# Modulation strips that hold whole sums, and the last gate made in the router's stage

## The chip, the cores and the metric

One NeuronCore of one Trainium2 chip runs the whole kernel in a single launch. The metric is the time of one execution on the device in microseconds (us); less is better. Five engines work beside each other: PE (TensorE, matmuls; its weight loads are listed as PEld), DVE (VectorE), ACT (ScalarE), POOL (GpSimd) and SP (SyncE, whose queue issues almost all the loads). They wait for each other through semaphores only.

## The reference, cut to what matters

256 tokens of 1024 channels pass through one layer of a hybrid trunk. All data are float32.

```python
c_act = silu(c)                                   # c: (1, 1024)
mod = c_act @ ada_w + ada_b                       # (1, 6144)
sh1, sc1, gt1, sh2, sc2, gt2 = split(mod, 6)      # 1024 each
h = rms_norm(x, norm1_g) * (1 + sc1) + sh1
proj = h @ w_in                                   # q k v g gk_low z xbc dt gates: 11,312 columns in all
o_a = gla_mixer(...)                              # gated linear attention, chunks of 64
o_b = ssd_mixer(...)                              # causal conv of xbc, Mamba-2 scan, chunks of 64
merged = gate_a * (o_a @ w_oa) + gate_b * (o_b @ w_ob)
x = x + gt1 * (merged @ w_out)
h = rms_norm(x, norm2_g) * (1 + sc2) + sh2
x = x + gt2 * hier_moe(h, ...)                    # top-1 group of 4, top-2 of its 8 experts, SwiGLU, width 256
return rms_norm(x, final_norm_g)
```

The modulation is twelve blocks of 512 columns: 0 and 1 are sh1, 2 and 3 sc1, 4 and 5 gt1, 6 and 7 sh2, 8 and 9 sc2, 10 and 11 gt2.

## The kernel before, in words

**Weights** come in pieces of 1 MB (128 partitions x 2048 floats) in the order of the list `PIECES`. SP issues them in order (line 427) into a ring of five slots (`LOADS`), and each issue waits until the piece five places earlier has been used (`piece_used`). After them SP issues 96 expert pieces (three per expert, line 422) into sixteen slots (`moe_slots`): parts of buffers that are free by then, among them the eight ring slots. Expert piece j waits for the reader of piece j - 16. SP's queue is in order, so an issue that waits holds back all behind it.

**Split products.** A weight of the trunk is used as a rounded high part (ACT, line 567) and a low part (DVE, line 858), and each product is three matmuls in float32r. `SPLITS` lists the pieces that are split; a modulation piece is not. ACT and DVE split two pieces ahead of the point at which they stand (`AHEAD`, `before`).

**Order on PE.** The order is written out by hand: `sumsq`; the first four modulation blocks (`ADA_FIRST`, pieces loaded beside the ring into free buffers, `EARLY`); eight units `xbc` of 512 channels with the convolution on DVE; `k`, `q`, `v` (2), `g` (2), `z` (4), `gate` (4), `oa` (2), `ob` (2), `out` (2); the router; the experts. `project` does a unit: 96 matmuls of 256 columns where the output is channel-major, 48 of 512 where it is token-major (`k v g z out`). `ADA_AFTER` says behind which unit a modulation block stands. `keep_clock(n)` issues n matmuls of ones that nobody reads.

**A modulation block.** `modulation(i)` multiplies silu(c), repeated 32 times as a 32-column weight, with the two pieces of block i, 256 columns each. The eight k-steps of a piece go to four 32-row strips of one PSUM bank, so each strip holds the sum over two of the eight k-steps. ACT copies the bank to SBUF (`ada_out`, line 581). `modulation_columns(i)` then multiplies the copy by a column of ones in four matmuls, which adds the strips and turns the row into four columns of 128 channels; DVE scales these by 1/32 and adds `ada_b` (`modulation_out`, line 865). gt1 and gt2 are needed as rows: `modulation_rows(w)` makes diagonal matrices of the columns (DVE), PE multiplies ones by them (`gtb`), DVE copies. The rows of gt2 end in `gt2_two`, two halves of 64 rows, which scales the output of each expert.

**Small columns.** Behind `xbc` 0 PE makes `small`: the 16 columns of gk_low transposed (8 matmuls of 256 columns with a 16-column weight) and the 32 columns of dt (16 matmuls of 32 columns). `acum` (8 matmuls of 32 columns) and `gklin` (2 of 512 columns) stand behind `k`.

**Around the router.** After `out` 1 PE makes the logits, then `keep_clock(22)`; DVE works out the choices (lines 1183 to 1218) and releases `mask_ok`; PE makes `pos` (5 matmuls), `keep_clock(8)`, then `select_first_quad`, which gathers the rows of the first four experts, and `up_of(0)`. From there each expert is `up_of`, `turn_of`, `select_quarter`, `down_of`.

The small PSUM results (`MIX`) share banks 4 to 7 in turn, in the order of `PLAN`: `begin(name)` waits for the reader of the result four places earlier.

## Time and profile before

| | us |
|---|---|
| median of 3 runs (lowest to highest) | 741.28 (739.49 to 741.56) |
| the profiled execution, whole | 742.72 |
| its span in the trace | 740.9 |
| PE busy | 705.9 (95%) |
| DVE busy | 400.8 (54%) |
| ACT busy | 265.3 (36%) |
| mean traffic | 277 GB/s over the span |

The span is what the trace shows from the first to the last record of the core; 1.8 us of the execution lie around it.
### The profile page before, as it was taken

What the parts mean: (1) busy time and instruction counts of PE and PEld (TensorE: products, weight loads), DVE (VectorE), ACT (ScalarE), POOL (GpSimd) and SP (SyncE); (2) the same over time, 40 slices, a digit from 0 to 9 for tenths busy, and PEclk for the clock granted to TensorE, in tenths of its full rate; (3) what the DMA queues carried; (4) which work ended last, traced back from release to release, by engine and by line L of the source; (5) the groups of instructions that cost most, each with busy time, mean ns of one, the idle gap of its engine ahead of it and who ended that gap; (6) DMA issues with size and microseconds to landing.
All of it is one profiled execution on the core that took longest, in us unless ns stands there. A gap on an engine that the chain in (4) does not pass through costs nothing.

```text
span 740.9 us, 13185 instructions
## 1 busy us (share of the span) xinstructions
PE 705.9 (95%) x5600; PEld 570.0 (77%) x5600; DVE 400.8 (54%) x691; ACT 265.3 (36%) x375; POOL 66.6 (9%) x66
## 2 busy tenths in 40 slices
PE   9899999999999999999999999999999999997892
PEld 7689999989777777799998999886566666655541
DVE  3386778764675556997877456463423122121226
ACT  3245545547446244343635334222131122121001
POOL 0010000000000170440000000001111111111110
PEclk9998999999999999999999999999999999999997
DMA  9964647655776535334354447988999999999971
GB/s 367 416 220 178 236 169 284 229 187 220 256 281 228 192 118 173 132 126 136 113 196 148 171 168 270 423 341 313 407 416 418 418 421 420 420 419 420 420 296 58
DMA packets 30893, 200.48 MB, mean 271 GB/s; under 512 B 4999, under 2 KB 5383, under 8 KB 7410
## 3 DMA queue, kind: packets, MB, share of 16 engines
q1 hardware_dynamic: 27506, 193.01, 67.6%
q0 software_dynamic: 3328, 6.62, 2.4%
q8 instruction: 45, 0.74, 0.4%
q14 instruction: 14, 0.11, 0.0%
HBM read 194.57 MB, written 10.75 MB: 277 GB/s over the span
## 4 chain that ended last, share of the span: by engine, by line
PE 79%; DMA 11%; DVE 5%; ACT 2%; issue 2%; SPq 1%; DVEq 0%; ACTq 0%
PE ps L1446 77%; DMA ring<-in_expert_pieces 7%; DMA r_btm<-in_pieces 2%; DVE ring_rounded L858 1%; DMA ring<-in_pieces 1%; ACT ring_rounded L567 1%; PE ps L1566 1%; PE ps L1859 1%; SPq L422 1%; DVE r_kq L1067 0%; DVE r_xs_rounded L1130 0%; DVE x_sb L1402 0%; DVE x_sb L1429 0%; DVE x_sb L1421 0%; DVE r_kq L1061 0%
## 5 line engine op out<-in xcount | busy, mean ns | idle before, releaser
L858 DVE TENSOR_TENSOR ring_rounded<-ring,ring_rounded 128x2048 fp32r<-128x2048 f32 x60 | 138.0, 2304 | 91.4 <-ACT ring_rounded L567 91.2
L1446 PE MATMUL ps<-hT_rounded,ring_rounded 128*128 128x256 f32 x832 | 157.0, 289 | 0.9 <-DVE x_sb_rounded L897 0.9
L567 ACT CAST ring_rounded<-ring 128x2048 fp32r<-128x2048 f32 x60 | 114.2, 1904 | 70.2 <-DMA ring<-in_pieces 40.6
L1446 PEld LDWEIGHTS ps<-hT_rounded,ring_rounded 128*128 128x128 f32 x832 | 133.7, 196 | 4.1 <-issue 3.9
L1446 PE MATMUL ps<-x_sb_rounded,ring_rounded 128*128 128x256 f32 x416 | 119.4, 287 | 0.0
L1446 PE MATMUL ps<-ring_rounded,hT_rounded 128*128 128x512 f32 x352 | 109.5, 392 | 0.0
L1446 PEld LDWEIGHTS ps<-x_sb_rounded,ring_rounded 128*128 128x128 f32 x416 | 81.6, 196 | 0.2 <-issue 0.2
L1446 PEld LDWEIGHTS ps<-ring_rounded,hT_rounded 128*128 128x128 f32 x352 | 65.3, 188 | 14.9 <-issue 1.7
L1446 PE MATMUL ps<-ring,r_lm 128*64 128x256 f32 x512 | 65.4, 380 | 3.1 <-DMA ring<-in_expert_pieces 3.1
L1446 PEld LDWEIGHTS ps<-ring,r_lm 128*64 128x64 f32 x512 | 42.8, 137 | 27.1 <-issue 12.3
L788 ACT ACTIVATE sq<-ps 128x128 f32<-128x128 f32 x32 | 8.9, 277 | 147.9 <-PE ps L1446 147.9
L530 POOL DMA_INDIRECT y_rows<-r_st,r_btm x29 | 28.4, 980 | 355.4 <-DVE r_st L1333 355.4
L1333 DVE TENSOR_TENSOR r_st<-ps,r_kq 128x512 f32<-128x512 f32 x32 | 22.1, 691 | 65.1 <-PE ps L1446 65.1
L1446 PE MATMUL ps<-ring_rounded,x_sb_rounded 128*128 128x512 f32 x144 | 56.1, 390 | 0.0
L1309 DVE TENSOR_SCALAR r_btm<-ps,par 128x1 int32<-128x1 f32 x29 | 6.2, 219 | 79.4 <-PE ps L1859 79.4
L1446 PE MATMUL ps<-r_lm_rounded,ring_rounded 128*128 128x256 f32 x256 | 46.2, 283 | 0.0
L779 ACT ACTIVATE r_lm<-ps,mod 128x256 f32<-128x256 f32 x60 | 30.5, 560 | 43.5 <-PE ps L1446 43.5
L1446 PEld LDWEIGHTS ps<-r_lm_rounded,ring_rounded 128*128 128x128 f32 x256 | 40.0, 192 | 0.0
L934 DVE SCALAR_TENSOR_TENSOR r_lm<-r_lm,par 128x255 f32<-128x255 f32 (+2 forms) x96 | 39.1, 476 | 0.0
L1446 PE MATMUL ps<-r_xs_rounded,ring_rounded 128*128 128x256 f32 x128 | 36.2, 283 | 0.0
L1446 PE MATMUL ps<-r_pv_rounded,r_ct_rounded 128*128 128x256 f32 x128 | 33.8, 301 | 0.0
L520 POOL TENSOR_TENSOR r_v<-r_xs,dtb 128x512 f32<-128x512 f32 x8 | 11.3, 1409 | 239.9 <-DVE r_st L1020 205.0
(308 smaller groups left out, 1125.3 us busy)
## 6 DMA issues: line engine op xcount, KB each, us to landing
ring<-in_pieces SPq DMA_DIRECT2D x76, 1024.0 KB, 5.0
ring<-in_expert_pieces SPq DMA_DIRECT2D x48, 1024.0 KB, 20.2
r_z<-in_expert_pieces SPq DMA_DIRECT2D x12, 1024.0 KB, 16.2
r_xs<-in_expert_pieces SPq DMA_DIRECT2D x12, 1024.0 KB, 17.3
g_sb<-in_expert_pieces SPq DMA_DIRECT2D x6, 1024.0 KB, 17.9
r_st<-in_expert_pieces SPq DMA_DIRECT2D x6, 1024.0 KB, 19.0
r_bt<-in_expert_pieces SPq DMA_DIRECT2D x6, 1024.0 KB, 23.1
hT<-in_expert_pieces SPq DMA_DIRECT2D x6, 1024.0 KB, 22.6
```

The costliest lines, as they stand in the source:

```text
L422: sp.dma_start(moe_slots[j % MOE_SLOTS], expert_pieces[j]).then_inc(moe_full[j % MOE_SLOTS], 16)
L520: link(nc.gpsimd.tensor_tensor(heads(xdt[:, b, t]), heads(src[:, t]), over(dt[:, t, h], SP_), ALU.mult))
L530: pool.indirect_dma_start(out=y_rows[:, :], out_offset=bass.IndirectOffsetOnAxis(ap=idx_i[:, e:e + 1], axis=0), in_=y_row[:, e % 2], in_of ...
L567: nc.scalar.copy(high_of(p_), slot_of(p_)).then_inc(hi_ok, 1)
L779: ins = nc.scalar.activation(hsel[:, m // 4 % 2, k].rearrange("p e r -> p (e r)"), ps[m if m < 4 else 4 + m % 4][:, a * 4 * W:(a + 1) * 4 ...
L788: nc.scalar.activation(hid_s[:, e % 2], ps[e % 2][:, 0:P], ACT.Silu).then_inc(silu_up, 1)
L858: nc.vector.tensor_tensor(low_of(p_), slot_of(p_), high_of(p_).bitcast(F32), ALU.subtract).then_inc(lo_ok, 1)
L934: ins = nc.vector.scalar_tensor_tensor(acc[:, a, tap:], u[:, a, 0:T - tap], w, acc[:, a, tap:], ALU.mult, ALU.add)
L1333: nc.vector.tensor_tensor(y_row[:, e % 2], ps[2 + e % 2][:], gt2_two, ALU.mult).then_inc(y_out, 1)
L1446: return nc.tensor.matmul(o, l, r, start=start, stop=stop)
L1566: ins = nc.tensor.transpose(bank[:, at:at + P], src, ident)
L1859: nc.tensor.transpose(ps[e % 2][:, 2 * P:3 * P], hid[:, e % 2], ident).then_inc(turned, 1)
```

## The change

- `modulation`: a piece now holds 512 rows of the weight and all 512 columns of the block, its columns reordered by the host. Each of four k-steps is four matmuls of 128 columns, one into each strip, and the two pieces accumulate into the same strips: strip j holds the whole sum of its 128 columns. It is 32 matmuls of 128 columns in place of 16 of 256.
- `ada_out` and `modulation_columns` go. DVE transposes the 128x128 result in 32x32 blocks straight from PSUM and adds `ada_b` to every 32nd column.
- Blocks 4 to 9 stand behind `xbc` 0 to 5. Blocks 10 and 11 are no longer made there, nor are `gtb` of gt2 and its diagonal matrices.
- gt2 becomes `gate_rows(q)`, q = 0 to 3: four pieces of 256 rows x 1024 columns, each four matmuls of 512 columns with a 64-column weight (`c_half`) into two 64-row strips of one bank. Three of them replace `keep_clock(22)`, the fourth replaces `keep_clock(8)`. DVE adds the bias into `gt2_two` after `low_part(1)`.
- The four gate pieces are the last of `PIECES`. Expert pieces 0 to 2 are issued earlier, among the loads for `ob`; the expert slots are put in another order, and slots 12 to 15 come free when the gate pieces have been read.
- The start is reordered: the halves of the modulation blocks and of the first unit alternate, with other counts of `keep_clock`.
- `small` is one group of 16 matmuls of 48 columns; gk_low is turned by two transposes behind `xbc` 3, where `acum` now is too, as 4 matmuls of 64 columns; `gklin` is behind `xbc` 5; the log-sigmoid works on both halves at once.

```diff
 
 
-ADA_AFTER = {("xbc", 2): 4, ("xbc", 4): 5, ("xbc", 6): 6, ("k", 0): 7, ("q", 0): 8, ("v", 0): 9, ("v", 1): 10,
-             ("g", 0): 11}
+ADA_AFTER = {("xbc", i): 4 + i for i in range(6)}
 ADA_FIRST = [2, 0, 3, 1]
-ADA_ORDER = ADA_FIRST + list(range(4, 12))
+ADA_ORDER = ADA_FIRST + list(range(4, 10))
...
+GATE_ROWS = [("gt", q, 0, 0) for q in range(4)]
+PIECES += GATE_ROWS
 PIECE_AT = {p_: i for i, p_ in enumerate(PIECES)}
 EARLY = [("ada", i, h, 0) for i in ADA_FIRST for h in range(2)]
...
-    [PIECE_AT[_p] % LOADS] + [LOADS + SPLIT_AT[_p] % HIGHS] * (_p in SPLITS[-HIGHS:]))]
+RING_FREED = [(LOADS + SPLIT_AT[_p] % HIGHS, _p) for _p in SPLITS[-HIGHS:-1]]
+RING_FREED += [(PIECE_AT[SPLITS[-1]] % LOADS, SPLITS[-1]), (LOADS + SPLIT_AT[SPLITS[-1]] % HIGHS, SPLITS[-1])]
+RING_FREED += [(PIECE_AT[_p] % LOADS, _p) for _p in GATE_ROWS]
 
 PIECES_OF = {}
...
-            for n, p_ in list(enumerate(PIECES))[1:]:
+            def load_piece(n, p_):
                 if n >= LOADS:
                     piece_used(sp, PIECES[n - LOADS])
                 sp.dma_start(slot_of(p_), piece_src(p_)).then_inc(slot_full[slot_at(n)], 16)
+
+            for n, p_ in list(enumerate(PIECES))[1:-4]:
+                if n >= LOADS and PIECES[n - LOADS] == ("oa", 1, 0, 0):
+                    mix_wait(sp, ("obT", 7))
+                    load_moe(0)
+                    load_moe(1)
+                    for h in range(2):
+                        sp.dma_start(gt2_two[h * W:(h + 1) * W], gate_bias[h].partition_broadcast(W)).then_inc(s_wr, 16)
+                if n >= LOADS and PIECES[n - LOADS] == ("ob", 0, 0, 0):
+                    for h in range(2):
+                        unit_wait(sp, ("oa", 1), h)
+                    load_moe(2)
+                load_piece(n, p_)
                 if n == 1:
                     sp.dma_start(wsm, small_w).then_inc(s_small, 16)
                     sp.dma_start(wgk2, gk2_rows).then_inc(s_small, 16)
...
-            load_moe(0)
-            load_moe(1)
-            for h in range(2):
-                unit_wait(sp, ("oa", 1), h)
-            load_moe(2)
             for h in range(2):
...
             load_moe(5)
-            for n, (_, p_) in enumerate(RING_FREED):
-                piece_used(sp, p_)
+            at_gate = PIECE_AT[GATE_ROWS[0]]
+            for q in range(3):
+                load_piece(at_gate + q, GATE_ROWS[q])
+            piece_used(sp, RING_FREED[0][1])
+            load_moe(6)
+            load_piece(at_gate + 3, GATE_ROWS[3])
+            for n in range(1, 4):
+                piece_used(sp, RING_FREED[n][1])
                 load_moe(6 + n)
             for t in range(TT):
                 unit_wait(sp, ("out", 1), t)
-            load_moe(14)
-            load_moe(15)
+            load_moe(10)
+            load_moe(11)
+            for q in range(4):
+                piece_used(sp, GATE_ROWS[q])
+                load_moe(12 + q)
             for j in range(MOE_SLOTS, 3 * E):
                 e, part = divmod(j - MOE_SLOTS, 3)
...
-                    ada_out(11)
 
             def gla_squares():
                 for t in range(TT):
@@ -727,6 +733,8 @@
                         unit_used(("gate", i), h), 1)
                 if i < 3:
                     ssd_squares(i + 1)
+                if i == 2:
+                    nc.scalar.copy(c_half, over(col("c", 0, 8), W)).then_inc(c_done, 1)
                 if i == 1:
...
 
             def modulation_out(i):
                 if i >= 4:
-                    before(("adc", i))
-                bank = mix_wait(dve, ("adc", i))
-                nc.vector.scalar_tensor_tensor(mod[:, 4 * i:4 * i + 4], bank[:, 0:4], 1.0 / 32, col("ada_b", 4 * i, 4), ALU.mult,
-                                               ALU.add).then_inc(mix_used(("adc", i)), 1)
+                    split_to(PIECES_OF["ada", i])
+                bank = mix_wait(dve, ("ada", i))
+                turned_ = ada_turned[:, i % 2]
+                nc.vector.transpose(turned_.rearrange("p m c -> p (m c)"), bank[:, 0:P]).then_inc(mix_used(("ada", i)), 1)
+                mix_taken(dve, ("ada", i))
+                link(nc.vector.tensor_tensor(mod[:, 4 * i:4 * i + 4], turned_[:, :, 0], col("ada_b", 4 * i, 4), ALU.add))
 
             nc.vector.memset(gkT, 1.0).then_inc(ones_done, 1)
             bank = mix_wait(dve, "sumsq")
...
                             step += 1
                         else:
                             ins.then_inc(conv_done, 1)
-                if g % 2 == 0 and ("xbc", g // 2 - 2) in ADA_AFTER:
-                    modulation_out(ADA_AFTER["xbc", g // 2 - 2])
-            modulation_out(6)
-
-            before("acum")
-            bank = mix_wait(dve, "acum")
-            nc.vector.tensor_copy(acum, bank[:, 0:64].rearrange("p (t h) -> p t h", t=TT))
-            nc.vector.tensor_copy(dend, bank[:, 64:128].rearrange("p (t h) -> p t h", t=TT))
-            nc.vector.tensor_copy(cdec[:].rearrange("p c h -> p (c h)"), bank[:, 128:256]).then_inc(mix_used("acum"), 1)
+                if g == 8:
+                    before("gkT")
+                    bank = mix_wait(dve, "gkT")
+                    dve.wait_ge(ones_done, 1)
+                    nc.vector.tensor_copy(gkT[0:RANK, :], bank[0:RANK, 0:T]).then_inc(mix_used("gkT"), 1)
+                    bank = mix_wait(dve, "acum")
+                    nc.vector.tensor_copy(acum, bank[:, 0:64].rearrange("p (t h) -> p t h", t=TT))
+                    nc.vector.tensor_copy(dend, bank[:, 64:128].rearrange("p (t h) -> p t h", t=TT))
+                    nc.vector.tensor_copy(cdec[:].rearrange("p (t a) h -> p a t h", a=2), bank[:, 128:256].rearrange(
+                        "p (a t h) -> p a t h", a=2, t=TT)).then_inc(mix_used("acum"), 1)
+                if g == 12:
+                    for t in range(TT):
+                        before(("gklin", t))
+                        bank = mix_wait(dve, ("gklin", t))
...
             pick_quad(0)
             low_part(1)
+            bank = mix_wait(dve, "gt2")
+            nc.vector.tensor_tensor(gt2_two, bank[:], gt2_two, ALU.add).then_inc(mix_used("gt2"), 1)
+            mix_taken(dve, "gt2")
             for m in range(4):
                 dve.wait_ge(sel_full, m + 1)
                 k = 2 * m + 1
...
-                for h in range(2):
+            def modulation(i, halves=(0, 1)):
+
+                for h in halves:
+                    bank = mix(("ada", i))[0] if h else begin(("ada", i))
                     p_ = ("ada", i, h, 0)
                     loaded(pe, p_)
-                    for k in range(KD):
-                        j = k % 4 * 32
-                        ins = mm(bank[j:j + 32, h * HC:(h + 1) * HC], c_wide[:, k], slot_of(p_)[:, k], k < 4, k >= 4)
+                    rows_ = slot_of(p_).rearrange("p a b -> p (a b)").rearrange("p (k n) -> p k n", n=CW)
+                    for k in range(KD // 2):
+                        for j in range(4):
+                            ins = mm(bank[32 * j:32 * j + 32, 0:P], c_wide[:, h * KD // 2 + k], rows_[:, k, j * P:(j + 1) * P],
+                                     h == 0 and k == 0, h == 1 and k == KD // 2 - 1)
                     ins.then_inc(full(("ada", i)) if h else ada_read, 1)
-                    keep_clock(then_keep[h] if then_keep else 0)
-
-            def modulation_columns(i):
-
-                mix_taken(pe, ("ada", i))
-                bank = begin(("adc", i))
-                for m in range(4):
-                    ins = mm(bank[:, m:m + 1], ada_sum[:, ADA_ORDER.index(i) % 2, m * P:(m + 1) * P], ones[:, 0:1])
-                ins.then_inc(full(("adc", i)), 1)
 
             def split_product(o, l, r, start, stop):
 
...
                 ins = mm(bank[:, 0:T], ones, x_sqT[:, k], k == 0, k == KD - 1)
             ins.then_inc(full("sumsq"), 1)
             pe.wait_ge(c_done, 1)
-            modulation(ADA_FIRST[0], 6, 2)
-            modulation_columns(ADA_FIRST[0])
-            keep_clock(2)
-            modulation(ADA_FIRST[1], 8, 0)
-            modulation_columns(ADA_FIRST[1])
+            modulation(ADA_FIRST[0])
+            keep_clock(4)
+            modulation(ADA_FIRST[1], (0,))
+            keep_clock(32)
+            modulation(ADA_FIRST[1], (1,))
+            keep_clock(6)
+            modulation(ADA_FIRST[2], (0,))
             keep_clock(8)
-            first_half_of_first_unit()
-            modulation(ADA_FIRST[2])
-            modulation_columns(ADA_FIRST[2])
-            modulation(ADA_FIRST[3], 2, 0)
-            modulation_columns(ADA_FIRST[3])
-            keep_clock(12)
+            modulation(ADA_FIRST[2], (1,))
+            first_half_of_first_unit(0)
+            modulation(ADA_FIRST[3], (0,))
+            first_half_of_first_unit(1)
+            modulation(ADA_FIRST[3], (1,))
+            keep_clock(16)
             for i in range(8):
                 project(("xbc", i))
                 if i == 0:
 
                     pe.wait_ge(s_small, 32)
                     bank = begin("small")
-                    for k in range(KD):
-                        mm(bank[0:RANK, 0:T], wsm[:, k, 0:RANK], h_f[:, k], k == 0, k == KD - 1)
+                    n_sm = RANK + SH
...
                         for k in range(KD):
-                            ins = mm(bank[:, T + t * SH:T + (t + 1) * SH], h_f[:, k, t * P:(t + 1) * P], wsm[:, k, RANK:], k == 0,
-                                     k == KD - 1)
+                            ins = mm(bank[:, t * n_sm:(t + 1) * n_sm], h_f[:, k, t * P:(t + 1) * P], wsm[:, k], k == 0, k == KD - 1)
                     ins.then_inc(full("small"), 1)
 
                 if 1 <= i <= 6:
...
-                    modulation_columns(ADA_AFTER["xbc", i - 1])
+                if i == 3:
+                    pe.wait_ge(gk_tm_ok, 1)
+                    bank = begin("gkT")
+                    for t in range(TT):
+                        ins = nc.tensor.transpose(bank[0:RANK, t * P:(t + 1) * P], gk_tm[:, t], ident)
+                    ins.then_inc(full("gkT"), 1)
+                    pe.wait_ge(dA_done, 1)
+                    bank = begin("acum")
+                    mm(bank[:, 0:TT * SH], upto, dA.rearrange("p t h -> p (t h)"))
+                    mm(bank[:, 64:64 + TT * SH], after, dA.rearrange("p t h -> p (t h)"))
+                    for a in range(2):
+                        ins = mm(bank[:, 128 + a * TT * SH:128 + (a + 1) * TT * SH], inch[:, a], dA.rearrange("p t h -> p (t h)"))
+                    ins.then_inc(full("acum"), 1)
+                if i == 5:
...
-            bank = begin("acum")
-            for t in range(TT):
-                mm(bank[:, t * SH:(t + 1) * SH], upto, dA[:, t])
...
@@ -1788,7 +1782,21 @@
                 for k in range(KD // 2, KD):
                     ins = mm(logits[t][:, 0:36], x2T[:, k, t * P:(t + 1) * P], wrs[:, k], False, k == KD - 1)
                 ins.then_inc(full(("router", t)), 1)
-            keep_clock(22)
+            def gate_rows(q):
+                p_ = GATE_ROWS[q]
+                loaded(pe, p_)
+                rows_ = slot_of(p_).rearrange("p a b -> p (a b)").rearrange("p (k n) -> p k n", n=D)
+                bank = mix("gt2")[0]
+                for k in range(2):
+                    for h in range(2):
+                        ins = mm(bank[h * W:(h + 1) * W, :], c_half[:, 2 * q + k], rows_[:, k, h * CW:(h + 1) * CW],
+                                 q == 0 and k == 0, q == 3 and k == 1)
+                ins.then_inc(full("gt2") if q == 3 else gate_read, 1)
+
+            pe.wait_ge(c_done, 2)
+            begin("gt2")
+            for q in range(3):
+                gate_rows(q)
             pe.wait_ge(mask_ok, 1)
             bank = begin("pos")
...
@@ -1880,6 +1888,8 @@
                 for j in range(4):
                     even(j, 1, 1, False, True).then_inc(sel_even, 1)
                 for j in range(4):
+                    if 4 + j == mix("gt2")[1]:
+                        mix_taken(pe, "gt2")
                     k = 2 * j + 1
                     for t in range(TT):
                         for n_, part in enumerate(h2_parts):
@@ -1888,7 +1898,7 @@
                                      t == TT - 1 and n_ == 1)
                     ins.then_inc(sel_full, 1)
 
-            keep_clock(8)
+            gate_rows(3)
             select_first_quad()
             up_of(0)
...
     for n, (kind, i, h, r) in enumerate(EARLY + PIECES):
         w, at = (of[kind], 0) if kind in of else (w_in, OFF[kind])
-        if kind in TOKEN_MAJOR:
+        if kind == "gt":
+            pieces[n] = by_partition(of["ada"][i * D // 4:(i + 1) * D // 4, 10 * CW:12 * CW]).reshape(P, KD, HC)
+        elif kind in TOKEN_MAJOR:
             pieces[n] = by_partition(w[h * D // 2:(h + 1) * D // 2, at + i * CW:at + (i + 1) * CW]).reshape(P, KD, HC)
+        elif kind == "ada":
+            cols = w[h * D // 2:(h + 1) * D // 2, i * CW:(i + 1) * CW].reshape(D // 2, 4, 4, 32).transpose(0, 2, 1, 3)
...
```

## Rows read from the trace of the kernel before

**Rows 1.** By windows, late in the experts; last columns clock, DMA share, GB/s.

```profile
660.00:700.00 40.00, 33.54 (x269) 21.95 (x269) 7.94 (x25) 5.46 (x13) 4.88 (x5) 1.00 1.02 420
```

**Rows 2.** Chain of waits in order of time: start, us, what.

```profile
71.09 11.51 PE ps L1446 x96
...
83.47 13.57 PE ps L1446 x128
...
97.91 12.41 PE ps L1446 x104
...
672.89 27.09 DMA ring<-in_expert_pieces
```

**Rows 3.** Timeline, the start: start, us, engine, line, operation.

```profile
10.93 1.07 PE L1446 MATMUL ps<-r_v,r_st 128*32 128x256 f32 x16
...
19.98 1.07 PE L1446 MATMUL ps<-r_btm,r_st 128*32 128x256 f32 x16 [0.15 <-DMA r_btm<-in_pieces]
...
39.45 0.36 PE L1446 MATMUL ps<-hT_rounded,ring_rounded 128*128 128x256 f32 x1
```

**Rows 4.** Groups of PE by form, whole span: busy us, mean ns.

```profile
L1446 PE MATMUL ps<-ring,r_pv 128*64 128x512 f32 x128 | 31.0, 604 | 1.9 <-issue 1.9
L1446 PE MATMUL ps<-ring,r_st 128*32 128x256 f32 x256 | 15.5, 382 | 0.0
...
L1446 PE MATMUL ps<-r_v,r_lm 64*64 64x64 f32 x256 | 8.3, 220 | 0.0
```

**Rows 5.** Timeline of PE behind the first convolution unit.

```profile
48.25 8.15 PE L1446 MATMUL ps<-r_z 128*16 128x256 f32 x48
56.21 0.56 PE L1446 MATMUL ps<-hT_rounded,ring_rounded 128*128 128x256 f32 x1
```

**Rows 6.** By windows, the two low-clock stretches; the clock stands third from the end.

```profile
56.00:62.00 6.00, 6.00 (x31) 6.00 (x32) 2.30 (x6) 3.58 (x4) 0.00 (x0) 0.55 0.46 184
170.00:174.00 4.00, 4.00 (x21) 4.00 (x22) 1.36 (x3) 3.25 (x4) 0.00 (x0) 0.57 0.86 360
```

**Rows 7.** Timeline of PE behind `k` (first row) and behind `gate` 2 (second).

```profile
166.09 1.97 PE L1446 MATMUL ps<-dtb,par 128*128 128x32 f32 x16
...
365.41 1.88 PE L1446 MATMUL ps<-r_pv,ones 128*128 128x512 f32 x4
```

**Rows 8.** Waits, 200 to 320 us: us in total, times, longest.

```profile
PE ps L1446 <- DVE mod L865: 2.8, 2, 1.5
```

**Rows 9.** Timeline, the router's stage.

```profile
482.50 5.16 PE L1446 MATMUL ps<-ones 128*128 128x128 f32 x44
...
482.86 0.41 DVE L1183 SCALAR_TENSOR_TENSOR r_btm<-ps,st,r_btm 128x36 f32<-128x36 f32 x2
...
487.75 0.63 PE L1446 MATMUL ps<-r_btm,par 128*128 128x32 f32 x4
...
490.68 0.36 PE L1446 MATMUL ps<-r_pv_rounded,r_ct_rounded 128*128 128x256 f32 x1
```

**Rows 10.** Timeline of SP's queue, the third expert load that waits for a used slot.

```profile
507.62 0.33 SPq L422 DMA_DIRECT2D g_sb<-in_expert_pieces  x1
```

**Rows 11.** By windows, the loads before and at the first experts, columns as in Rows 1.

```profile
395.00:455.00 60.00, 59.62 (x494) 59.11 (x494) 34.84 (x36) 23.92 (x23) 0.00 (x0) 1.00 0.45 157
455.00:495.00 40.00, 39.42 (x248) 35.00 (x247) 26.53 (x61) 13.45 (x21) 0.00 (x0) 1.00 1.01 421
...
495.00:500.00 5.00, 4.57 (x40) 3.60 (x40) 1.99 (x8) 0.00 (x0) 0.00 (x0) 1.00 0.33 138
...
505.00:510.00 5.00, 5.00 (x39) 2.86 (x39) 1.36 (x6) 1.02 (x2) 0.75 (x1) 1.00 0.46 136
```

**Rows 12.** The page: a part of sections 5 and 6.

```profile
L858 DVE TENSOR_TENSOR ring_rounded<-ring,ring_rounded 128x2048 fp32r<-128x2048 f32 x60 | 138.0, 2304 | 91.4 <-ACT ring_rounded L567 91.2
...
L567 ACT CAST ring_rounded<-ring 128x2048 fp32r<-128x2048 f32 x60 | 114.2, 1904 | 70.2 <-DMA ring<-in_pieces 40.6
...
ring<-in_pieces SPq DMA_DIRECT2D x76, 1024.0 KB, 5.0
```

162 lines of the change are left out of this document (62 added, 100 removed).

## The prediction, made before the changed kernel was run

> **What bounds the kernel now.** I read the windows first. Late in the experts the DMA engines are busy all the time (1.02 of them at 420 GB/s) while PE has work for 33.5 of 40 us [rows 1], and the chain of waits goes over an expert load for 27 us there [rows 2]. So the end is set by the loads. But they don't bound the trunk: from 395 to 455 us the DMA engines are 45% busy, PE 59.6 of 60 us; from 455 on they are full while the sixteen slots fill, and between 495 and 510 they pause twice, because nothing is free to load into [rows 11]. The second pause ends at 507.62, when `down_of(0)` frees slot 2 [rows 10]. From there 78 expert pieces are queued without a gap at some 2.5 us each (1.049 MB at 420 GB/s [rows 1]). The end is therefore the time of `down_of(0)` plus a constant, and `down_of(0)` is the end of a PE-bound trunk. The rule for the sum is: each us that PE's queue loses ahead of the first expert is a us at the end, as long as the pauses remain; what PE does beside the later experts counts for nothing.
>
> In the chain the `xbc` stage is pure PE: 11.51 us for a unit alone, 13.57 with the products of a modulation block, 12.41 with its column sums [rows 2]. So a block costs 2.06 + 0.90 = 2.96 us of PE.
>
> **The change part by part.** All in us, minus is faster.
>
> *The start, -1.7.* The new order is counted from 10.93, where the first products begin [rows 3]. A half block is 1.07 (16 records of 256 columns; I take the same for 32 of 128) [rows 3], a matmul of `keep_clock` two records of 0.117 (44 in 5.16) [rows 9]. Block 2 to 13.1, keep 4 to 14.0, half a block to 15.1, keep 32 to 22.6, half to 23.7, keep 6 to 25.1, half 26.1, keep 8 to 28.0, half 29.1, then half a unit matmul group (12 x 0.12 = 1.4) 30.5, half 31.6, group 33.0, half 34.1, keep 16 to 37.9. The load that ends last for block 0 is there at 20 [rows 3], before 22.6. The second half of the first unit began at 39.45 [rows 3]; it is now PE's turn at 37.9, while the channels' path from the last sum (transpose, add, h, high and low part, some 3) is ready at 37.2. Gain 1.6 to 1.7; if the count is off by a keep or by the path, 0.5 to 2.7.
>
> *`small`, -4.1.* It took from 48.25 to 56.1: 48 records [rows 5]. It becomes 32 records, each with a full weight load, so 0.117 as for the ones [rows 9], 3.75. Between 0.107 and 0.14 each: -4.4 to -3.4.
>
> *Six blocks behind `xbc`, -5.1.* The column sums go (-0.90), with ACT's copy. The products are 64 records of 128 columns for 32 of 256, four strips side by side. Before, 15.5/256 = 0.060 a record; half the columns give 0.030 if columns set the pace, and 0.060 if the record does. Small records in strips are shown: 256 of 64 columns in 8.3, or 0.032 each [rows 4]. I take 0.033: 2.1 a block in place of 2.96, six times -0.85. Ends: 0.027 (1.7 a block, -7.4) and 0.060 (3.9 a block, +5.5). DVE gets a transpose (no row has one; a 128x512 pass is 0.7, so 0.2 to 0.7) and an add; it loses nothing on the path, as DVE waits for ACT's high parts [rows 12].
>
> The Trainium skill (TensorE: Matmul & The Clock Gate, "Wait — 56ns, not 53.3ns?") gives some 62 ns for each matmul when the queue is decoded in software; by that the block would be 64 x 0.062 = 4.0. The row of 0.032 speaks against it [rows 4].
>
> *Blocks 10 and 11 and the rows of gt2, -7.6.* Two blocks leave the trunk (-5.9), and the two products by diagonal matrices: 4 records from 365.41, 1.7 until the next unit streams [rows 7]. That they go is certain; what they cost later is the gate step below.
>
> *`acum`, `gklin`, gk_low, -0.8.* 16 records in 1.97 [rows 7] become 8 (-1.0), two transposes come (+0.2). `gklin` only moves. Both need data of DVE that are long there, two units later.
>
> *Waits behind `g`, -2.0.* PE stood 2.8 before the GLA updates for `modulation_out` of blocks 10 and 11 [rows 8], which waited behind DVE's low part. The waiting instruction is gone; a part can return as a wait for the same low parts, so I take 2.0 (0 to 2.8).
>
> *Clock, -2.2.* The granted clock falls to 0.5 (1.2 GHz) twice: behind `small`, and behind block 7, `acum` and `gklin` in a row; the mean is 0.55 over 6 us and 0.57 over 4 [rows 6], a loss of 2.7 + 1.7 = 4.4. Both runs of narrow matmuls are shorter now or broken up: 7.9 us becomes 3.75 followed by a block, 5.9 us is spread over three places. But the same change puts blocks next to `acum` (4.2 us in all) and `gklin` (4.9). I count half back; 0 to 4.4. The Trainium skill (same page, "HAM oscillation — how this bites in real kernels") lays the fall to half speed to stretches in which PE waits; here it fell with PE busy throughout, in narrow work [rows 5, 6]. By the page the 2.2 would not be to be had, and the sum would be 721.4.
>
> *The gate rows, +1.4.* Four pieces of 8 records of 512 columns with a 64-column weight; such a record is 31.0/128 = 0.242 [rows 4]. Their bank comes free with DVE's first read of the logits, at 483.1; three pieces last 5.8, until 488.9. `pos` could start at 487.75 [rows 9], so it is 1.2 late. The fourth piece is 1.94 for the 2.0 of keep 8, but `select_first_quad` could start at 490.68 [rows 9] only as PE came free; now PE is free at 492.1. +1.4; 0.8 to 2.5. DVE's add (0.7) falls beside the first twelve gather matmuls, and the bank is wanted only behind the sixteenth.
>
> *The loads, 0.* That no load comes late must be checked, since 4.2 MB move from a half-idle stretch into a full one. From 455 on: expert pieces 3 to 11 (nine), four gate pieces, 12 to 17 (six): 19 x 2.5 = 47 us, where before it was pieces 0 to 17, 45 us, and two pauses. Pieces 0 to 2 move to 403 to 417, where there is room: the DMA engines idle for 33 us between 395 and 455 [rows 11]. In order of release: gate 0 after `ob` 1, gates 1 and 2 and piece 6 after `out` 0, gate 3 and piece 7 at 472, 8 to 11 by 478, landing until 489.5; 12 to 14 when the gates are read (485 to 489), 15 at 492, 16 and 17 at 500.5, landed at 507.5; piece 18 is released at 509.0. So one pause is filled, the other is left with 1.5 us, and the end still hangs on `down_of(0)`. The bound from the other side: each 2.5 us of pause that I counted wrongly is 2.5 late, at most two of them, +5.
>
> The loads for `ob` get two pieces and a bias ahead of them, 6 us. A piece lands 5.0 after its issue and needs 1.9 and 2.3 for its parts [rows 12]; the piece released at 402 is then ready at 418 and used at 423. In the `xbc` stage each unit now has four pieces in 14.5 us, 10 us of traffic; a piece's slot is released 14.5 us before PE needs it, and the way is 9.2: 5 to spare. Cover that goes would show as PE waiting for a low part.
>
> **Sum.** -1.7 - 4.1 - 5.1 - 7.6 - 0.8 - 2.0 - 2.2 + 1.4 = -22.1. Against the profiled execution (742.7, of which the span is 740.9) that is 720.6; against the median of 741.3, which is 1.4 under it, 719.2.
>
> **Rivals.**
>
> *A, the loads take part of it:* the full DMA stretch before the first expert becomes gapless and piece 18 comes late by one or two transfers. For it: 19 transfers in a stretch that had two short pauses. Against: 33 us of room further ahead. Time 719.2 + 2.5 to 5: 723.
>
> *B, a record costs 0.060 whatever its columns:* six blocks +0.9 in place of -0.85 each (+10.5), and five half blocks on the start's path (+0.9 each, +4.5). For it: every record of the trace in a 32-row strip streams 256 columns, so none shows that a shorter one is cheaper. Against: 0.032 for 64 columns. Time 734. The 62 ns of the Trainium skill's page would give the same within 1 us.
>
> *C, all comes out at its good end:* no low clock (-2.2), all waits gone (-0.8), 0.030 a record (-1.1). Time 715.
>
> *D, slower: the clock.* If every cluster of narrow work (six behind `xbc`, one at the start) drops the clock for the 6 to 7 us that it took at 56 to 62, each costs some 2.7 to 3.3, seven of them 19 to 23, and the 2.2 counted back are lost: 719.2 + 2.2 + 22 = 743. It decides from six drops on. For it: two drops in the trace, in such work. Against: the blocks behind `xbc` 2 and 4 ran at full clock, and 13.57 - 11.51 leaves no room for one.
>
> **Chances.** The forecast 0.62 (its own range 716 to 723), A 0.14, C 0.12, B 0.08, D 0.03, that parts of the change don't act at all 0.01. The likeliest is 719.2. The range takes in C and A and the near part of B: 713 to 729. A difference under 0.3% (2.2 us) can't be told from none here. Faster by more 0.95, the same 0.02, slower 0.03.
>
> **What would show it.** The timeline: the second half of the first unit near 37.9; `small` near 3.8 long; a unit with its block 13.6 apart from the transposes; no wait for DVE behind `g`; `pos` 1.2 behind `mask_ok`; the first gather some 21 us ahead of 490.7. The windows: clock 1.00 through the trunk but for at most one stretch; DMA share 1.0 from a pause before slot 2 is freed to the end. The prediction is wrong if the shift of the first `down_of` and that of the end differ (A), or if a block takes over 3 us (B).

## The result: slower, 748.3 us against 740.6

Over four runs of each, the changed kernel took 748.32 us (745.95 to 752.24) and the kernel before 740.58 (739.49 to 741.56): a ratio of 1.0111, 95% interval 1.0069 to 1.0152. The forecast was 719.2. The profiled execution is 746.2 us with a span of 744.3. Medians are compared with medians and spans with spans below: a profiled execution can lie at either edge of its own runs.

The start is where it was forecast: the second half of the first unit begins at 38.13 (39.45 before [rows 3]). By windows of the changed kernel, columns as in [rows 1], TensorE then loses ground that it had before. The first row is the end of the experts, the next four are in the trunk, the last two around the first expert.

```profile
660.00:700.00 40.00, 35.69 (x294) 23.75 (x290) 6.66 (x21) 6.76 (x16) 4.88 (x5) 1.00 1.02 420
...
60.00:80.00 20.00, 15.45 (x164) 14.61 (x163) 11.00 (x20) 8.50 (x10) 0.00 (x0) 0.91 0.67 257
...
100.00:120.00 20.00, 16.69 (x165) 15.68 (x164) 10.91 (x21) 6.01 (x8) 0.00 (x0) 0.83 0.59 211
120.00:140.00 20.00, 17.79 (x190) 16.37 (x188) 14.74 (x32) 8.25 (x9) 0.00 (x0) 1.00 0.63 218
...
180.00:190.00 10.00, 1.33 (x6) 1.36 (x7) 4.90 (x3) 6.79 (x8) 0.00 (x0) 0.58 0.33 107
...
484.00:488.00 4.00, 3.45 (x15) 1.75 (x16) 3.41 (x18) 2.19 (x2) 0.00 (x0) 0.67 1.00 416
495.00:500.00 5.00, 4.62 (x36) 3.89 (x32) 3.32 (x6) 1.93 (x4) 0.00 (x0) 1.00 1.01 419
```

TensorE is missing 4.6 us from 60 to 80, 3.3 from 100 to 120, 2.2 from 120 to 140 and 8.7 from 180 to 190; before, it was busy for the whole of each 20 us between 40 and 200. The end is as it was, full DMA engines at 420 GB/s [rows 1], and the two pauses of the loads at 495 and 505 [rows 11] are filled now (share 1.01 in the row, and 0.97 from 505 to 510). Piece 18 (`g_sb`) is released at 512.5 in place of 507.62 [rows 10], 4.9 later, and the span is 3.4 longer. So the rule of the forecast (what the trunk loses is lost at the end) held within 1.5 us, with the other sign: the first expert begins at 500.31 where it was 495.44, also 4.9 later. Which instructions TensorE waits for, from 40 to 240 us of the changed kernel (waited-for line: us in total, times, longest):

```profile
PE ps L1452 <- DVE ring_rounded L866: 9.6, 1, 9.6
PE ps L1564 <- issue: 4.5, 1, 4.5
PE ps L1452 <- DVE r_st L874: 4.1, 2, 3.3
PE ps L1564 <- DVE r_z L958: 2.2, 1, 2.2
PE ps L1452 <- DVE r_lm L1006: 1.1, 1, 1.1
```

The `issue` line names no releaser. In the kernel before, the whole list for this stretch was one wait of 1.4 us. The first four lines, 20.4 us, are in two places.

**The `xbc` stage.** The `issue` line is TensorE in front of the transposes of unit 0. What comes first is to be seen on ScalarE, here from the timeline of the changed kernel in unit `xbc` 3 (start, us, line, in brackets the idle time before and its releaser):

```profile
96.31 1.90 ACT L591 CAST ring_rounded<-ring 128x2048 fp32r<-128x2048 f32 x1 [7.77 <-DMA ring<-in_pieces]
98.11 0.58 ACT L631 COPY r_lm<-ps 128x512 f32<-128x512 f32 x1
```

L591 splits a weight piece, and it stands ahead of L631, the copy of a unit's bank, since `before(unit, half)` splits up to two pieces ahead (`AHEAD`) first. The piece is the first of the next unit, `xbc` 4. With four pieces a unit and five slots, it takes the slot of the block just ended (the one behind `xbc` 2): its load is issued at 87.7, as the block's last product is done, and is there 8.55 us later (the chain of waits, below). The bank's half is full 5.8 us after the unit's start. So the copy waits for a load that TensorE itself needs only 14.4 us after its issue (unit 11.5, transposes 0.9, block 2). The forecast had 5.0 us from issue to landing; this load, the third issued within 3 us, took 8.6, and the one behind the first block 11.7. Behind the copy come VectorE's convolution (3.1 us), SiLU, the transposes, and the reads by VectorE of blocks and sums that free the next banks (L874, L958). The chain goes just this way, from the block behind `xbc` 2 to the products behind `xbc` 3 that start late:

```profile
85.79 1.93 PE ps L1452 x64
87.73 8.55 DMA ring<-in_pieces
96.31 1.91 ACT ring_rounded L591
...
101.18 2.36 DVE r_lm L944 x6
103.91 5.56 PE ps L1452 x72
```

Over 60 to 160 us, ScalarE's own waits in the kernel before and in the changed one:

```profile
ACT ring_rounded L567 <- DMA ring<-in_pieces: 24.6, 10, 5.0
```
```profile
ACT ring_rounded L591 <- DMA ring<-in_pieces: 46.5, 9, 11.2
```

**In front of `q`.** From the timeline of the changed kernel, ScalarE and then VectorE:

```profile
179.12 0.58 ACT L653 COPY r_kq<-ps 128x512 f32<-128x512 f32 x1 [0.33 <-PE ps L1452]
179.72 1.28 ACT L655 ACT_TABLE_LOAD   x1
181.01 1.06 ACT L655 ACTIVATE r_pv<-r_pv 128x1024 f32<-128x1024 f32 x1
...
182.72 1.28 ACT L660 ACT_TABLE_LOAD   x1
```
```profile
171.85 1.22 DVE L978 SCALAR_TENSOR_TENSOR r_pv<-g_sb 128x1024 f32<-128x1024 f32 x1
185.10 1.23 DVE L980 SCALAR_TENSOR_TENSOR g_sb<-g_sb,r_pv 128x1024 f32<-128x1024 f32 x1 [12.04 <-ACT r_pv L660]
186.25 4.48 DVE L866 TENSOR_TENSOR ring_rounded<-ring,ring_rounded 128x2048 fp32r<-128x2048 f32 x2
```

VectorE had the decay gate's absolute value at 173.1. ScalarE took it at 181.0, behind both copies of `k`, and VectorE waited 12 us for the logarithm while the low part of `q`'s first piece stood behind that wait; TensorE had finished `k` and waited 9.6 us for it. In the kernel before, ScalarE's logarithms stood behind the copies of `k` as well. But there VectorE's reads of `acum` and `gklin` stood just ahead of its wait for them, and `before("acum")` ahead of those reads made the low parts of both pieces of `q` first:

```profile
159.22 2.29 DVE L858 TENSOR_TENSOR ring_rounded<-ring,ring_rounded 128x2048 fp32r<-128x2048 f32 x1 [2.92 <-ACT ring_rounded L567]
165.71 2.29 DVE L858 TENSOR_TENSOR ring_rounded<-ring,ring_rounded 128x2048 fp32r<-128x2048 f32 x1 [4.19 <-ACT ring_rounded L567]
173.31 0.69 DVE L964 SCALAR_TENSOR_TENSOR g_sb<-g_sb,r_pv 128x512 f32<-128x512 f32 x1 [2.64 <-ACT r_pv L645]
```

The change moved these reads into the `xbc` stage, and the splits that stood in front of them went with them. It also put both halves of the log-sigmoid into one step, and took away the 5.9 us of products between `k` and `q` (164.0 to 169.9 before: block 7, `acum`, `gklin`). ScalarE's rows also show a load of the tables for Exp and one for Ln. The Trainium skill (ScalarE: Activation LUTs, "Table sets: the hidden batching unit") has Ln and Exp in one set, one load for both; here it was two, 2.6 us.

### The profile page after: what moved, and what is told of

It is laid out like the page before. It is cut to its first block, busy times and chain, and to the rows that moved or that the text cites. A ratio compares the mean times of both kernels' runs of the same rounds, so it can differ in the third digit from the quotient of the medians.

```text
span 744.3 us, 13476 instructions
## 1 busy us (share of the span) xinstructions
PE 693.3 (93%) x5758; PEld 562.3 (76%) x5758; DVE 400.6 (54%) x695; ACT 255.8 (34%) x361; POOL 66.4 (9%) x66
## 4 chain that ended last, share of the span: by engine, by line
PE 75%; DMA 12%; DVE 6%; ACT 3%; issue 3%; SPq 0%; DVEq 0%; ACTq 0%
PE ps L1452 73%; DMA ring<-in_expert_pieces 8%; DMA ring<-in_pieces 3%; DVE ring_rounded L866 2%; DMA r_ct<-in_pieces 2%; ACT ring_rounded L591 2%; PE ps L1564 1%; PE ps L1867 1%; DVE r_lm L944 1%; DVE r_lm L1006 0%; DVE r_kq L1077 0%; DVE r_xs_rounded L1133 0%; DVE x_sb L1408 0%; DVE x_sb L1435 0%; DVE x_sb L1427 0%
## 5 line engine op out<-in xcount | busy, mean ns | idle before, releaser
L1452 PE MATMUL ps<-hT_rounded,ring_rounded 128*128 128x256 f32 x832 | 155.3, 287 | 9.6 <-DVE ring_rounded L866 9.6
L591 ACT CAST ring_rounded<-ring 128x2048 fp32r<-128x2048 f32 x60 | 114.2, 1904 | 104.6 <-DMA ring<-in_pieces 67.4
L1452 PEld LDWEIGHTS ps<-hT_rounded,ring_rounded 128*128 128x128 f32 x832 | 131.9, 193 | 12.7 <-issue 12.7
L1452 PE MATMUL ps<-ring,r_lm 128*64 128x256 f32 x512 | 72.7, 380 | 3.0 <-DMA ring<-in_expert_pieces 3.0
L1452 PEld LDWEIGHTS ps<-ring,r_lm 128*64 128x64 f32 x512 | 46.4, 137 | 27.3 <-issue 12.6
L1339 DVE TENSOR_TENSOR r_st<-ps,r_kq 128x512 f32<-128x512 f32 x32 | 22.1, 692 | 65.0 <-PE ps L1452 65.0
L544 POOL TENSOR_TENSOR r_v<-r_xs,dtb 128x512 f32<-128x512 f32 x8 | 13.3, 1666 | 245.4 <-PE ps L1452 236.5
## 6 DMA issues: line engine op xcount, KB each, us to landing
g_sb<-in_expert_pieces SPq DMA_DIRECT2D x6, 1024.0 KB, 17.1
```

The lines of the kernel that those rows point to most:

```text
L544: link(nc.gpsimd.tensor_tensor(heads(xdt[:, b, t]), heads(src[:, t]), over(dt[:, t, h], SP_), ALU.mult))
L591: nc.scalar.copy(high_of(p_), slot_of(p_)).then_inc(hi_ok, 1)
L1339: nc.vector.tensor_tensor(y_row[:, e % 2], ps[2 + e % 2][:], gt2_two, ALU.mult).then_inc(y_out, 1)
L1452: return nc.tensor.matmul(o, l, r, start=start, stop=stop)
```

## The experiments

All times are medians, with the lowest and the highest run, and then the ratio to runs of the kernel before on the same chip with its 95% interval. "The span fell" compares profiled executions, with the changed kernel's 744.3 where nothing else is said.

**e1_spread: the blocks back, everything else of the change kept.**

```
-ADA_AFTER = {("xbc", i): 4 + i for i in range(6)}
+ADA_AFTER = {("xbc", 2): 4, ("xbc", 4): 5, ("xbc", 6): 6, ("k", 0): 7, ("q", 0): 8, ("v", 0): 9}
```

> Whole-sum strips, start, early sums, joint log-sigmoid and gate rows as in the changed kernel; only the six late modulation blocks go back behind units xbc 2, 4, 6, k, q, v0. Theory (the blocks behind each of the first six units make the ring of five slots too short: ScalarE's split waits for a load and holds up the bank copy queued behind it, so TensorE stalls for 4.5, 3.3, 2.2 and some smaller waits): the stalls between 60 and 160 us go, 10 us; one block behind k covers 2 us of the 9.6 us wait in front of q. Expected 748 - 12 = 736 us. Rival (the loads and splits have room wherever the blocks stand, and the stalls come from the wider sums or from the vector transposes): 745 to 750 us with the same stalls.

732.4 us (731.4 to 733.9), ratio 0.9887 [0.9859, 0.9915]. From 60 to 160 us no wait of TensorE is left in the list at all; from 40 to 240 it is, beside 2.7 for the rows of sums of `v`,

```profile
PE ps L1457 <- DVE ring_rounded L866: 10.0, 2, 9.0
```

The wider `small`, the turned sums and the early `acum` are all still there, so the stalls of the `xbc` stage come from the place of the blocks. The span fell by 12.3. The block behind `k` took only 0.6 from the other wait (9.0 in place of 9.6), where the theory had 2.

**e2_gk: the log-sigmoid ahead of the copies of `k`.**

```
-            for t in range(TT): ... copy of k's bank t
+            before((("k", 0), 0))
             act.wait_ge(gk_in, 1)
             ... Exp, the three small Exps, Ln ...
+            for t in range(TT): ... copy of k's bank t
 (VectorE)
+            before((("k", 0), 0))
             dve.wait_ge(gk_l, 1)
```

> The changed kernel, but ScalarE makes the joint log-sigmoid of the decay gate (Exp, Ln) ahead of its two copies of unit k, and VectorE makes the low part of q's first piece ahead of its wait for that logarithm. Theory (the 9.6 us TensorE wait in front of unit q is the low part queued on VectorE behind the logarithm, which ScalarE reaches only after k's banks): the wait falls to 1 us or less and the clock stays up there: 748 - 9 = 739 us, the xbc stage unchanged. Rival (the wait in front of q is for the load of q's pieces): no change, 748 us.

735.8 us (730.3 to 739.7), 0.9934 [0.9908, 0.9960]; the span fell by 8.0, the median by 12.5 (the runs of this kernel scatter over 9 us, and the profiled one, 738.2, is above the median). The 9.6 us wait is gone and the clock is 1.00 from 160 to 200. The stalls of the `xbc` stage stay (the third, 1.8, is not shown):

```profile
PE ps L1454 <- DVE r_st L875: 5.3, 2, 2.9
PE ps L1566 <- issue: 4.3, 1, 4.3
```

The edit does two things, the logarithm earlier and the low part ahead of the wait for it. No run has one of them alone.

**e3_zero: the 2 MB of zeroing later.**

```
-            unit_wait(pool, ("xbc", 0), 1)
             for i in range(ZERO_PARTS):
+                unit_wait(pool, ("xbc", 2 + i), 1)
                 pool.dma_start(zero_rows[i * P:(i + 1) * P, :], zeros)...
```

> The changed kernel, but the four parts of the zeroing of the expert rows in memory (2 MB, issued together behind the first unit at 48 us) go out one each behind units xbc 2, 3, 4 and 5. Theory A (the 4.5 us stall at 64 us comes from the loads that share the DMA engines with the zeroing, 8.9 and 11.7 us from issue to landing): that stall goes, the later ones stay: 748 - 4 = 744 us. Rival (the ring alone is too short, the zeroing has no part in it): the stall at 64 stays, 748 us, or the four parts make the later stalls longer, 750 us.

746.1 us (746.0 to 746.8), 1.0079 [1.0053, 1.0104], the span 744.3, the changed kernel's own. The first stall shrank and those at VectorE's reads grew from 4.1 (the third, 2.1, is not shown):

```profile
PE ps L1452 <- DVE r_st L874: 5.3, 2, 3.3
PE ps L1564 <- issue: 2.3, 2, 1.6
```

So both theories had a part of it: the zeroing shapes the first stall, but it is not what makes the stage late.

**e4_order: the blocks where they are, the splits one piece ahead instead of two.**

```
-                    before((("xbc", i), half))
+                    before((("xbc", i), half), 1)      # and so on VectorE, and for small, tr, gkT, gklin
 (VectorE, ahead of the decay gate; two pieces ahead had this piece split by then)
+            split_to(PIECES_OF[("k", 0), 1])
```

> The changed kernel with all its blocks where they are, but in the xbc stage ScalarE and VectorE split a piece one piece ahead instead of two before they take a unit's bank, so that a late load holds up no bank copy. Theory (the load is late, but TensorE stalls because the copy, the convolution and the turned tiles behind it are late): 6 to 8 of the 10 us of stalls in the xbc stage go, 741 us. Rival (the loads themselves are too late for TensorE, whatever the order): TensorE waits as long for low parts of the ring instead, 748 us or slower.

736.9 us (734.8 to 739.2), 0.9953 [0.9934, 0.9972]; the span fell by 9.3, the median by 11.4. From 60 to 160 us ScalarE's waits and from 40 to 160 all of TensorE's are now

```profile
ACT r_lm L631 <- PE ps L1453: 44.5, 12, 6.7
ACT ring_rounded L591 <- DMA ring<-in_pieces: 6.6, 4, 3.2
```
```profile
PE ps L1453 <- DVE ring_rounded L866: 3.1, 3, 1.7
```

The same blocks in the same places, the same loads: of over 10 us of stalls, 3.1 are left, now for low parts. ScalarE waits for TensorE, as it should, and hardly for loads (6.6 in place of 46.5). This separates the order of the queues from the loads. Of the 3.1, the first wait (1.7, in front of `xbc` 2) stands behind a load, one of 11.6 us; the second (1.2, in front of `xbc` 7) stands in the chain of waits of e8, which has the same one, behind VectorE's convolution. So the loads themselves were late by 1.7 of the 10.8 us.

One piece ahead has a price of its own, just outside these windows: TensorE waits 0.3 in front of `k` and 2.6 in the middle of it, at 163.3, which the changed kernel did not. The chain of e8 below shows why.

**e5_spread_gk: e1 and e2 together.**

> Both repairs on the changed kernel: the six late blocks behind xbc 2, 4, 6, k, q, v0, and the joint log-sigmoid ahead of ScalarE's copies of unit k with the low part of q's first piece ahead of VectorE's wait for it. Theory (two separate faults, each a queue held up by a wait placed ahead of TensorE's next operand): the 9.0 us wait in front of q that the spread kernel still has goes, and the low clock behind it: 732.4 - 9 = 723.5 us. Rival (the two repairs use the same slack, q's loads are late once the logarithm is not): 728 us or more.

727.2 us (724.8 to 727.4), 0.9827 [0.9803, 0.9851], 5 less than e1 and not 9 (the two profiled executions are 9.1 apart, but e5's is the fastest of its four and e1's the slowest). Waits of 4.1 us for low parts are left, 3.1 in front of `q` and 1.0 in `v`, which e1 had too, and 2.7 for the rows of sums.

```profile
PE ps L1459 <- DVE ring_rounded L867: 4.1, 2, 3.1
```

The time is near the rival's, but its mechanism (late loads) isn't there. By the timeline VectorE waits for the block behind `k` and makes `q`'s low part only then, since `modulation_out(7)` stands ahead of it; the low part runs from 158.88 and TensorE starts `q` at 161.32:

```profile
158.33 0.32 DVE L875 STREAM_TRANSPOSE r_st<-ps 128x128 f32<-128x128 f32 x1 [7.96 <-PE ps L1459]
```

**e6_router_clock: e5 with 14 more products of ones in the router stage.**

> The kernel with both repairs, and 14 more 128x128 products of ones in the router stage (8 ahead of the gate rows, 2 behind each of the three). Theory (the router stage of the changed kernel took 17.3 us against 15.7 in the spread kernel because the granted clock fell in it, 0.67 from 484 to 488): the stage stays at 15.7 + 14 x 0.06 = 16.5 us; 0.8 us less than the kernel with both repairs if that one's clock falls there, 0.8 us more if it doesn't. Rival (the difference is gate rows that wait for their loads): the stage gets 0.8 us longer either way.

728.4 us (727.5 to 729.2), 0.9842 [0.9816, 0.9868]. The stretch from the first router product to the first expert is 15.70 us in e5 (462.94 to 478.64) and 18.98 in e6 (462.77 to 481.75), with the clock at 1.00 in both. The expectation had the price wrong: a product of ones is two records of 0.117, so 14 of them are 3.3, which is what the stage grew by. The clock of e5 had not fallen, so the case of the theory could not be tested. The rival is settled by the list of TensorE's waits in e5's and in the changed kernel's router stage, which has no wait for a load.

**e7_no_gate_rows: e5 with the last gate as it was made before.**

```
-ADA_AFTER = {..., ("v", 0): 9}
+ADA_AFTER = {..., ("v", 0): 9, ("v", 1): 10, ("g", 0): 11}
-GATE_ROWS = [("gt", q, 0, 0) for q in range(4)]
+GATE_ROWS = []
...          # diagonal products, loads and keep_clock(22), keep_clock(8) as before
```

> The kernel with both repairs, but the last gate not made as rows: its two modulation blocks stand behind v1 and g0 again (whole-sum strips), the diagonal products again behind the last gate unit, 22 and 8 products of ones in the router stage. Theory (the gate rows save what was forecast, 2 blocks and the diagonal products 7.6 less the extra 1.0 to 2.5 in the router stage; whole-sum blocks are the shorter ones here, 2.16 us each): 5 us slower than the kernel with both repairs, 728.5 us. Rival (TensorE had waits behind v1 and g0 that the blocks covered, so nothing was saved): the same within 1 us or faster.

733.5 us (731.4 to 736.5), 0.9917 [0.9892, 0.9942]: 6.3 slower than e5, where the theory had 5. The two blocks and the diagonal products are 2 x 2.08 + 1.7 = 5.9 us of TensorE, less 0.95 in the router's stage (below): 4.9. The rest is waits that come back: 2.1 us more of them in the trunk than in e5, among them 0.6 for the read of block 11 and, in front of the rows of sums, this in place of e5's 2.7:

```profile
PE ps L1450 <- DVE r_lm L1000: 3.8, 1, 3.8
```

The gate rows are the largest single gain that was measured by itself. What they cost in the router's stage is read off the chain of waits. First e7, then the changed kernel, and e5, each from the first record behind the last transposes (x24) to the first expert's (last row):

```profile
464.17 5.47 PE ps L1450 x24
...
487.24 2.78 PE ps L1450 x23
```
```profile
474.72 5.47 PE ps L1452 x24
...
485.56 14.06 PE ps L1452 x74
500.31 1.70 PE ps L1452 x13
```
```profile
454.63 5.47 PE ps L1459 x24
...
462.94 1.98 PE ps L1459 x16
465.46 12.49 PE ps L1459 x74
478.64 1.48 PE ps L1459 x11
```

That is 23.07, 25.59 and 24.01 us; the kernel before had 23.06 (472.38 to 495.44), the same as e7. The same code takes 12.49 us at full clock and 14.06 where the clock fell (0.67 from 484 to 488 above; e2, e4 and e10 had it too, with 14.20, 14.18 and 14.04, while e1, e3, e8 and e9 had 12.48 or 12.49). So the rows cost 0.95, and the low clock another 1.6 when it comes. What decides that was not settled.

**e8_gk_order: e2 and e4 together, the blocks still behind the first six units.**

> The changed kernel with its blocks where they are, and both the log-sigmoid repair and the splits of the xbc stage only one piece ahead. Theory (two separate faults add up): 748.3 - 12.5 - 11.4 = 724 us, the blocks' place then costing at most the few us that loads are still late in the xbc stage, so some 3 us above the spread kernel with the repair, 727 us. Rival (with one piece ahead q's low part is late anyway): 733 us.

724.5 us (723.1 to 725.8), 0.9786 [0.9757, 0.9815]: the two faults add up, with not a block moved. By medians 12.5 + 11.4 gave 724.4; by spans it is 21.2 against 8.0 + 9.3, so the sum is good to a few us only. Waits for low parts of 5.8 us in four are left, and 1.1 for the rows of sums. They are e4's: 1.7 in front of `xbc` 2, 1.2 in front of `xbc` 7, 0.3 in front of `k` and 2.6 in it. From the chain of waits, the first and the last of them:

```profile
52.10 11.60 DMA ring<-in_pieces
...
68.17 11.75 PE ps L1455 x96
...
155.96 2.38 DVE r_lm L945 x6
158.90 1.90 ACT ring_rounded L591
160.82 2.30 DVE ring_rounded L867
163.17 30.55 PE ps L1455 x176
```

The 11.6 us load is issued as the block behind `xbc` 0 ends, beside the zeroing. With one piece ahead, ScalarE reaches `k`'s second piece only behind the last SiLU, and that waits for VectorE's last convolution. Behind this wait the clock falls once more (0.63 from 164 to 168).

**e9_all_three: e5, splits one ahead, VectorE's read of the block behind `k` later.**

```
-            modulation_out(7)
             dve.wait_ge(gk_l, 1)
             ... gk_done
+            modulation_out(7)
```

> The kernel with both repairs (six blocks behind xbc 2, 4, 6, k, q, v0; log-sigmoid early), and the splits of the xbc stage one piece ahead, and VectorE's read of the block behind k placed behind the decay gate's result instead of ahead of its wait for the logarithm. Theory (the 3.1 us wait in front of q's second piece that is left there is VectorE waiting for that block before it makes the low part): 1 to 3 us less than 727.2: 725 us; the one piece ahead changes nothing here, as there is no stall in the xbc stage. Rival (that wait is ScalarE's, which reaches the piece only behind both functions and k's copies): 727 us.

727.4 us (725.2 to 728.7), 0.9821 [0.9800, 0.9841]: the same as e5, the rival's number. But the wait in front of `q` is gone, as the theory had it (of `q`'s first piece, not its second). What took its place is the price of one piece ahead, which the theory put at nothing: 0.8 in front of `k` at 147.6 and 2.1 in it at 155.4, and 1.0 in `xbc` 1. So the waits for low parts went from 4.1 in two to 4.9 in four. The read of the block alone, without the splits one ahead, was not run.

**e10_hybrid: blocks behind `xbc` 2 to 6 and `k`, with e2 and e4, the block behind `k` read as in e9.**

> The six late blocks behind xbc 2 to 6 and k, log-sigmoid early, splits of the xbc stage one piece ahead. Theory (a block behind a unit costs a stall only where the load of its pieces meets other traffic, as behind the first unit beside the 2 MB of zeroing, or where the bank copy is queued behind the split; with the split one ahead and no block behind the first two units, 3 of the 5.8 us of waits for low parts that the kernel with log-sigmoid and order repaired still has go, and no block delays the sums' rows behind v0): 724.5 - 2.5 = 722 us. Rival (the remaining waits belong to the rate of four pieces a unit, wherever the blocks stand): 724.5 us or more.

724.0 us (721.2 to 725.0), 0.9766 [0.9745, 0.9788]. Against e8 it is 0.4 less, which can't be told from nothing. The profiled executions show two things that cancel: waits for low parts fell from 5.8 to 3.8 and the router's stage begins 1.9 earlier (453.09 in place of 454.97), but in it the clock fell (14.04 us in place of 12.48), and the first expert begins only 0.3 earlier. It is 2.3% faster than the kernel before and, by the two ratios, 3.4% faster than the changed one.

## Why the prediction was wrong

The mechanism of the gain was right, and two delays of the trunk were not in the sum. With both repaired and every block in its place (e8) the kernel takes 724.5 us, inside the range of the forecast and 5 above its number.

*"The loads, 0" failed in the `xbc` stage.* The step said: "a piece's slot is released 14.5 us before PE needs it, and the way is 9.2: 5 to spare. Cover that goes would show as PE waiting for a low part." It compared the release with TensorE's need alone. But ScalarE asks for the piece much earlier, two pieces ahead, and in its queue the bank copy stands behind. With the measured landing of 8.6 the way is 12.8 us, so this load was in time for TensorE (14.4) and late for ScalarE. The "9.2" was short as well: it took 5.0, the middle case, for the landing. With 5.0, ScalarE's part would have been ready at 94.6, 1 us behind the bank's half (an estimate from 87.7 + 5.0 + 1.9, and 87.7 + 5.8), in place of the 98.2 that it was. It didn't show as a wait for a low part either, but as waits for transposed sums and for banks: in the changed kernel 4.5 + 4.1 + 2.2. e1 (blocks away) takes them all out, e4 (order) all but 3.1; the spans are 12.3 and 9.3 shorter.

*"`acum`, `gklin`, gk_low, -0.8 ... Both need data of DVE that are long there" was half the step.* The part of the change that joined the two halves of the log-sigmoid, and that lies between `gklin` and its use, was in the diff and not priced. "`gklin` only moves" looked at what the moved products need, not at what stood in front of their reads on VectorE: the splits of `q`. The price was one wait of 9.6 us, and e2 takes 8.0 out of the span (12.5 by medians). That the products behind `k` went was cover lost too, but one block put back there took only 0.6 from the wait (e1).

*The clock, forecast -2.2.* At 56 to 62 us it no longer falls: from 30 to 60 us the granted clock is 1.00 (0.91 before). But it fell at four new places (68 to 74, 102 to 109, 180 to 190, 484 to 488). The first three begin in or behind waits of TensorE (4.5, 3.3 and 9.6 us); there the section of the Trainium skill that the forecast weighed (TensorE: Matmul & The Clock Gate, "HAM oscillation — how this bites in real kernels") agrees with the trace. With the stalls repaired (e8) the mean clock is 0.991.

*The other terms came out.* Start -1.3 (forecast -1.7). `small`: 3.7 us for its 32 records, -4.4 (-4.1). A unit with its block is 13.59 in e1 where a unit alone is 11.51 [rows 2], so 2.08 a block where it had been 2.96, -0.9 each (-0.85); rival B is out, since 384 strip records took 14.4 us, 0.037 each with the low clock in it. The router's stage pays 0.95 for the gate rows (1.4). That e7 minus e5, 6.3, is near the forecast's 7.6 - 1.4 = 6.2 is in part luck: the 7.6 has blocks of 2.96, e7's are the shorter ones, and returned waits fill the gap. Rival A is out: the end moved less than the first expert, not more. D, the one on the slower side, named the clock, which fell behind the waits and was not their cause: e8 has all six blocks behind `xbc` and one fall in the trunk.

*The balance.* The forecast was -22.1 against the profiled execution, with 0.8 us of the 2.8 of waits in the trunk [rows 8] left. For e8: its trunk has 6.9 us of such waits, +6.1. Its clock falls once, which costs some 1.7 (3 us at about half), so it gave back 2.7 of the 4.4 and not 2.2: -0.5. `small` and the blocks, 0.3 each: -0.6. Gate rows and start together: 0. That makes -17.1. The first expert begins 16.5 earlier (478.96 for 495.44), and the span, 723.1, is 17.8 shorter. For the changed kernel: 21.5 us of waits, +20.7; the clock costs some 7.8 (busy time of TensorE times what is missing of the clock) in place of the 2.2 that the forecast left, +5.6; -0.6. That makes +3.6, and the first expert begins 4.9 later. Both sums are estimates, good to 1 or 2 us. In both kernels the end comes 1.3 to 1.5 better than the first expert, which no term has.

What stays open is that, which of the two halves of e2's edit does the work, and when the clock falls: behind a wait of 2.1 us in `k` it stayed up in e9, behind one of 2.0 in e10 it fell, and in the router's stage it falls in four kernels and not in five.

The chance of "slower" (0.03) was wrong in kind: all rivals but one were sizes of terms, and none was a queue in which one wait holds up another engine's next operand.

## What to carry to other kernels

- A load's slack is the time from its release to the first instruction in any queue that waits for it, not to the engine that computes with it. Then ask what is queued behind that instruction. With in-order queues, splitting ahead is a risk when the ring is short: two pieces ahead cost 9 us of the span here. One ahead is not free either: at the end of the stage the next split then stands behind the last convolution, which cost 2 to 3 us in `k`. One ahead in the stage and two at its end was not run.
- A small read that moves takes along what is queued in front of it. Before it moves, write down what each engine does just ahead of it: here the reads of `acum` and `gklin` took `q`'s splits along, and 9.6 us of TensorE hung on them.
- A chain between engines that TensorE needs only later (log-sigmoid) goes ahead of copies that nobody waits for, and no engine should wait for it in front of the next unit's operand.

## What the runs showed of the hardware

- Records of 128 columns in 32-row strips take 0.031 us each at full clock (192 of them in 5.9 us in e8, 90 to 165), half of the 0.060 for 256 columns [rows 4].
- VectorE's `transpose` of a 128x128 f32 tile out of PSUM (blocks of 32x32) takes 0.31 us.

```profile
L874 DVE STREAM_TRANSPOSE r_st<-ps 128x128 f32<-128x128 f32 x10 | 3.1, 310 | 8.1 <-PE ps L1452 8.1
L1452 PE MATMUL ps<-ring,r_st 128*32 128x128 f32 x384 | 14.4, 313 | 0.1
```

- The same instructions in the router's stage ran at full clock in e1, e3, e5, e8 and e9 (12.48 or 12.49 us) and at a lower one in the changed kernel, e2, e4 and e10 (14.04 to 14.20).
- The clock fell to half behind a wait of TensorE of 2.0 us (e10, in `k`: 0.50 from 160 to 163).
- A 1 MB load took up to 11.7 us from issue to landing beside the 2 MB of zeroing (two issued at 51.6 and 52.5 took 8.9 and 11.7), against 5.0 for the middle one of the kernel [rows 12].
